# A hybrid decoder layer on eight cores: new start-up order and weight layouts, weight folds in two lanes, and a token mixer that begins inside the last FFN1 tiles

## The reference, cut to what matters

```python
def reference(x, c, w_ada, b_ada, ...):           # x (4, 8192, 1024) f32, D = 1024, D_FF = 2816
    mod = (silu(c) @ w_ada + b_ada).reshape(b, 9, D)      # shift, scale, gate for each of 3 sub-layers
    h = modulate(x, sh1, sc1)                             # layer norm without affine, * (1 + scale) + shift
    y = swiglu(h, ffn1_w_gate, ffn1_w_up, ffn1_w_down)    # (silu(h @ gate) * (h @ up)) @ down
    x = layer_norm(ALPHA * x + 0.5 * g1 * y, ln1_g, ln1_b)
    h = modulate(x, sh2, sc2)
    y = token_mix(h, w_in, attn_sinks, pool_w_mix, pool_scale, w_out)
                                                  # window-128 attention with sinks ++ causal pooling, @ w_out
    x = layer_norm(ALPHA * x + g2 * y, ln2_g, ln2_b)
    h = modulate(x, sh3, sc3)
    y = swiglu(h, ffn2_w_gate, ffn2_w_up, ffn2_w_down)
    return layer_norm(ALPHA * x + 0.5 * g3 * y, ln3_g, ln3_b)
```

## Time and profile before

| | |
|---|---|
| median of 3 runs | 2553.81 us (2540.72 to 2639.39) |
| the profiled execution's own time | 2549.48 us |
| its span on the slowest core (core 4) | 2547.9 us (the cores: 2518.9 to 2547.9) |
| PE busy | 2278.3 us, 89% of the span |
| DVE, ACT, POOL busy | 54%, 29%, 17% |
| mean granted PE clock, core 4 | 0.978 |

### The profile page before, as it was taken

One profiled execution on the slowest core, in us unless ns is written; L12 is line 12 of the kernel. 1 busy time (PEld: TensorE's weight loads), 2 busy tenths in 40 slices (PEclk: granted clock), 3 DMA queues, 4 the chain that ended last, 5 costly groups with the idle time before them and its releaser, 6 DMA issues.

```text
span 2547.9 us, 42339 instructions; the slowest of 8 cores (2518.9 to 2547.9 us)
## 1 busy us (share of the span) xinstructions
PE 2278.3 (89%) x14236; PEld 1286.2 (50%) x14360; DVE 1374.3 (54%) x2756; ACT 730.5 (29%) x1523; POOL 430.6 (17%) x422
## 2 busy tenths in 40 slices
PE   0069977988989999999789999999999999999997
PEld 0035543545545555565345555555555555555555
DVE  0064423442455533424767667776867676677654
ACT  0021211221221222212343334433333434343321
POOL 3100131222201110101111111202121111111111
PEclk9999989989999999999889999999999999999999
DMA  9963178997654311223515555454655555454556
GB/s 156 156 169 85 67 104 142 156 156 131 142 152 134 128 34 52 73 100 109 181 63 194 183 182 191 166 199 153 216 183 182 194 178 201 177 199 165 200 185 221
DMA packets 138358, 385.88 MB, mean 151 GB/s; under 512 B 19616, under 2 KB 71584, under 8 KB 116640
## 3 DMA queue, kind: packets, MB, share of 16 engines
q1 hardware_dynamic: 73152, 338.45, 39.2%
q0 software_dynamic: 64992, 44.70, 14.9%
HBM read 385.86 MB, written 56.11 MB: 173 GB/s over the span
## 4 chain that ended last, share of the span: by engine, by line
PE 74%; DMA 11%; DVE 5%; issue 5%; another core or an unknown queue 2%; POOL 1%; ACT 1%; SPq 0%; DVEq 0%; POOLq 0%; ACTq 0%
PE ps L1130 24%; PE ps L472 16%; PE ps L1153 12%; PE ps L539 8%; DMA t_arena<-ffn_w_down 4%; DMA t_arena<-w_ada 3%; PE ps L941 3%; PE ps L911 2%; PE ps L1061 2%; PE ps L1059 2%; DVE t_arena L647 2%; PE ps L426 2%; DMA scr_gu<-ffn_w_up 1%; DMA scr_win<-w_in 1%
## 5 line engine op out<-in xcount | busy, mean ns | idle before, releaser
L472 PE MATMUL ps<-t_arena 128*128 128x384 bf16 x3872 | 650.4, 330 | 20.8 <-DVE t_arena L463 16.1
L1130 PE MATMUL ps<-t_arena 128*128 128x384 bf16 (+1 forms) x3872 | 637.8, 322 | 1.8 <-DVE t_arena L410 1.8
L472 PEld LDWEIGHTS ps<-t_arena 128*128 128x128 bf16 x3872 | 378.5, 99 | 276.3 <-issue 36.2
L1130 PEld LDWEIGHTS ps<-t_arena 128*128 128x128 bf16 x3872 | 371.5, 98 | 243.6 <-issue 23.1
L386 ACT ACTIVATE t_arena<-t_arena,t_stt 128x1024 f32<-128x1024 f32 (+1 forms) x195 | 241.4, 1240 | 427.8 <-DVE t_stt L381 421.6
L379 POOL TENSOR_TENSOR t_stt<-t_stt,t_mhalf 128x1 f32<-128x1 f32 x195 | 114.1, 585 | 1440.8 <-DVE t_stt L378 1430.5
L463 DVE TENSOR_TENSOR t_arena<-ps,t_sg 128x384 bf16<-128x384 f32 x242 | 133.4, 556 | 367.1 <-PE ps L472 345.5
L539 PE MATMUL ps<-t_arena 128*128 128x512 bf16 x1413 | 319.6, 384 | 6.2 <-DVE t_arena L463 3.9
L1153 PE MATMUL ps<-t_arena 128*128 128x512 bf16 x1358 | 303.6, 379 | 3.1 <-issue 0.8
L495 POOL TENSOR_TENSOR t_arena<-t_arena 128x1024 f32<-128x1024 f32 x97 | 231.2, 2383 | 420.7 <-DVE t_arena L494 410.5
L375 DVE BATCH_NORM_STATS2 t_stt<-t_arena 128x6 f32<-128x512 f32 x390 | 269.4, 691 | 48.9 <-DMA t_arena<-x_c 24.1
(11 more groups left out here) (74 smaller groups left out, 1495.9 us busy)
## 6 DMA issues: line engine op xcount, KB each, us to landing
t_arena<-scr_gu SPq DMA_DIRECT2D x121, 1024.0 KB, 6.9
t_arena<-scr_d SPq DMA_DIRECT2D x44, 1024.0 KB, 5.6
t_arena<-x_c SPq DMA_DIRECT2D x66, 512.0 KB, 5.5
t_arena<-scr_x SPq DMA_DIRECT2D x65, 512.0 KB, 6.1
t_arena<-ffn_w_down SPq DMA_DIRECT2D x44, 512.0 KB, 4.6
scr_x<-t_arena SPq DMA_DIRECT2D x33, 512.0 KB, 3.3
t_arena<-scr_d SPq DMA_DIRECT2D x22, 768.0 KB, 4.5
out_c<-t_arena SPq DMA_DIRECT2D x32, 512.0 KB, 4.4
```

Of the source, the lines that this page charges most:

```text
L472: ins = e.matmul(bk.f[:, 0:T], lhsT=w.ap[:, kc, gu, s2 * 128:(s2 + 1) * 128], rhs=hT.ap[:, kc, 0:T], start=(kc == 0), stop=(kc == 7))
L1130: ins = e.matmul(bk.f[:, 0:T], lhsT=wv[:, kc, gu, s2 * 128:(s2 + 1) * 128], rhs=hTc.ap[:, kc, 0:T], start=(kc == 0), stop=(kc == 7))
```

## The change: what it does

1. **Layouts.** `w_ada`, `w_in`, `w_out` and both FFNs' gate and up weights arrive rearranged from the host, so that every weight DMA reads and writes long contiguous pieces: one DMA per chunk of gate and up instead of two, one cast for `w_in` instead of 17, 11 casts for FFN2 instead of 22.
2. **Start-up order.** The seven small constants go out on ACT's DMA queue instead of SP's. POOL issues 8 + 7 DMAs and then takes its first x^-0.5. Section 2 of `w_ada` loads after chunk 6, chunks 7 to 10 follow it. A block is loaded and its statistics taken before a destination buffer is free (`take_n2`, `box`). Six buffers instead of three take the rows of `ffn1_w_down`. Tile 0's down projection walks the 22 row blocks outermost in six PSUM banks (`down_first`), so it needs them one after another.
3. **Gate vector.** It is stored in plain order, element by element (1024 pieces of 4 bytes), so that the fold reads it with stride 1.
4. **Background.** The fold of `w_out` runs as a stream beside the sections; the fold of `ffn2_w_down` runs in two lanes; the casts begin after the last section. Consumers of background DMAs are placed as if the DMA landed 3 to 10 us later (`lag`). The model of DMA time is changed: separate queues, 285 KB/us alone, 150 KB/us beside another queue, at most 16 POOL DMAs outstanding.
5. **Mixer start.** `hTm0`, an own tile for the first mixer input, and other places for LN2's parameters and two of the x buffers let projections of tiles -1 and 0 stand among S9's gate and up matmuls and the first attention blocks among S9's down matmuls. Until FFN1 ends, one of the six weight buffers is free instead of three.

The core of the diff:

```diff
@@ Prog.emit
-            self.free_at[eng] = t + (0.9 if eng == "pool" else 0.1)
-            self.dma_at = max(self.dma_at, t) + op.nbytes / 280e3
-            self.fin[ev] = self.dma_at + 2.0
+            if eng == "pool":
+                if len(self.sw) >= 16:
+                    t = max(t, self.sw[-16])
+                self.free_at[eng] = t + 0.9
+            else:
+                self.free_at[eng] = t + 0.4
+            t0 = max(self.dma_at[eng], t)
+            busy = any(self.dma_at[o] > t0 for o in ENG if o != eng)
+            self.dma_at[eng] = t0 + op.nbytes / (150e3 if busy else 285e3)
+            self.fin[ev] = self.dma_at[eng] + 2.5
@@ load_small
-                yield dmaq("sp", dst, src, s_const, (), [B_const], 32768)
+                yield dmaq("act", dst, src, s_const, (), [], 4096)
@@ ada_section (gate)
-                yield dmaq("sp", scr_gate[gate], gtmp[:, gate, :], s_g, [B_g], [B_gd], 4096)
...
+                gd = scr_gate[gate].rearrange("a (j p) -> (a p) j", p=128)
+                yield Op("sp", lambda e: e.dma_start(out=gd, in_=gtmp[:, gate, :], allow_slow_non_contiguous=True), [B_g], [B_gd], 0.1, s_g, 262144)
@@ fold_op
-            return Op("dve", lambda e: e.scalar_tensor_tensor(out=v3(out), in0=v3(src), scalar=scale, in1=gview(gt), op0=ALU.mult, op1=ALU.mult),
-                      rd, wr, 1.25)
+            return Op("dve", lambda e: e.scalar_tensor_tensor(out=out, in0=src, scalar=scale, in1=gt.ap, op0=ALU.mult, op1=ALU.mult),
+                      rd, wr, 1.25, lag=lag)
@@ load_gu1
-                for gu in range(2):
-                    src = (wg[0], wu[0])[gu][:, j * 256:(j + 1) * 256].rearrange("(kc p) n -> p kc n", p=128)
-                    yield dmaq("pool", wgu[j].ap[:, :, gu, :], src, wgu[j].sem(), (), [wgu[j].buf] if gu == 0 else [], 1048576)
...
+                if j == 7:
+                    flags.add("gu1_some")
+                    yield from until("g1loads")
+                yield gu_load(j)
@@ bg_work
+            S.spawn(fold_wout(), 3)
             for sec, slot in ((3, 2), (4, 3), (6, 4), (7, 5)):
                 yield from ada_section(sec, adas, slot=slot)
+            yield from until("wout")
             yield from ada_section(8, adas, gate=2, gate_tile=gateb)
...
+            flags.add("ada_done")
+            for ln in range(2):
+                S.spawn(fold_wd2(ln), 3)
@@ casts
-            yield from until(("S0", "down", 1))
...
+            yield from until("ada_done")
+            jobs = [(scr_win, w_in, 5 << 20, None)]
             for j in range(NGRP):
...
+                jobs.append((scr_gu[j], wgu_d[1][j], 1 << 21, j))
@@ p1_main
-            yield from until("wd1_all", ("S0", "aT", 0, 21), ("S0", "aT", 1, 21))
-            for t in range(2):
-                yield from down1(t, aTs[t], "S0")
+            yield from down_first(aTs[0])
+            yield from until("wd1_all")
+            yield from down1(1, aTs[1], "S0")
@@ m_main
-            yield from until("att_mem", ("msc", 2), ("msc", 3))
-            S.spawn(m_pre(-1, [0], (("S9", "gu"),)), 2)
+            yield from until("casts", ("msc", 2), ("msc", 3), ("t1", 10, "hT"))
+            S.spawn(m_pre(-1, [0], ()), 2)
```

282 lines of the change are left out of this document (166 added, 116 removed).

## The result

The changed kernel takes **2564.9 us** (median of 13 runs), the kernel before 2543.4 us beside it. The ratio is 1.008, 95% interval 1.006 to 1.010, so it is no faster, rather 0.8% slower; forecast were 2381 us. Some executions of most kernels here, the one before too, run up to 17% longer with a lower granted clock on the cores of one die; the ratios, and the time given for cast_16k, leave these out, the other medians are of all executions. The busy times hardly moved against the earlier trace rows: PE is busy as long as before, and the time is again PE's idle time.

What follows compares the result with a forecast made beforehand. PE was taken as the bound, its 270 us of idle time and lower clock as the possible gain. 53 + 131 + 60 + 663 + 1472 = 2379 us of span, plus 1.6, gave 2381 us, range 2335 to 2450.

Steps and rivals of the forecast that it cites:

- What bounds the kernel: Whole kernel: PE is the bound, busy 2278 of 2548 us; to gain are its 270 us idle and lower-clock losses.
- Term 1: Start of S0, the first gate and up matmul: from 140.3 to 53 us, bounds 47 and 77.
- Term 2: S0's gate and up matmuls: 131 us, was 136.0.
- the gate vector: Its store as 1024 pieces in S0: 5 us, bounds 2.85 and 23, covered by PE's matmuls.
- Term 3: S0's down projections: 60 us, was 58.3; tile 2 begins at 244 us.
- Rival A: S0: the gate vector's store takes eight times as long, PE waits 9 to 13 us, 2392 us in all; chance 0.08.
- Term 4: Tiles 2 to 8 with the background work: 663 us, was 713.3, with 30 us of waits left; bounds 639 and 733.
- Rival B: Tiles 5 to 7: casts starve SP's transfers, x comes late, PE loses 40 to 60 us, about 2431 us; chance 0.15.
- Rival C: Tiles 2 to 8: lags and lanes do nothing, all 72 us of idle time stay, 2431 us; chance 0.10.
- Term 5: From S9 to the end: 1472 us, was 1500.0; mixer start hidden, second-half tiles stay at 119.65 us; bounds 1466 and 1500.
- Rival D: Second half: new DMA prices reorder FFN2's weight stream; 16 us lost per tile would cancel the gain; chance 0.05.
- The sum: Whole kernel: the five terms give a span of 2379 us, with 1.6 us added 2381 us, 6.8% less.

Runs made afterwards that it cites:

- cast_16k: The changed kernel with its 12 casts split into pieces of 16 KB read and 8 KB written: 2552.2 and 2555.6 us, two executions, no ratio.
- sem_only: gate_and_cast with an own semaphore for the first three constants and the first use of sinkt moved after tile 1's transposes: 2474.9 us.
- gate_contig: The changed kernel with the gate vectors' old HBM layout, 128 pieces of 32 bytes, the fold reading with a stride: 2524.5 us.
- cast_4k: The changed kernel with its 12 casts split into pieces of 4 KB read and 2 KB written instead of 64 and 32 KB: 2539.7 us.
- gate_and_cast: The changed kernel with both edits, gate_contig and cast_4k; base of several later kernels: 2498.7 us.
- paced: gate_and_cast with the same casts held back in the emitted order to places in tiles 5 to 8: 2464.1 us.
- all_five: gate_and_cast with paced, pn_lag, the first constants' own semaphore, later first use of sinkt, and tile 1's x in other buffers: 2416.9 us.
- gate_on_pool: all_five with the second and third gate vector stored and broadcast from POOL's queue instead of SP's: 2408.1 us.
- hard_pace: gate_on_pool with each cast waiting for the last matmul that stands ahead of it in the plan: 2402.1 us.
- late_lane: hard_pace with the second fold lane starting at tile 7 and both lanes drawing from one list of 22 folds: 2385.9 us.
- pn_lag: gate_and_cast with DVE's multiply of the attention weights planned at 2.1 us instead of 1.13, nothing else: 2478.1 us.

## Why the prediction was wrong, step by step

**What bounds the kernel** was right: PE's idle time was the whole of it, and all that the experiments gave back came from there.

**Term 1 (S0 at 53 us)** failed on a wait that I had not priced. "I take 53" counts w_ada and the first chunk, and both prices were good: w_ada landed at 40.7 us in sem_only (44 forecast), and chunks 7.0 us apart in the changed kernel and 6.2 in sem_only (6.5 forecast). It took for granted that DVE and ACT begin when x is there, as DVE did in the kernel before, at 7 us. But the change moved the first use of a constant ahead of the layer norms, and the seven constants share a semaphore and land one by one between w_ada's loads, the last at 29 us. With that wait gone S0 starts at 47. No row of the kernel before could show it, since the wait was not there; the new order of the lists could.

**Term 2 and the gate vector.** The store cost 22 us on core 3 and 16.1 on core 4. I had bounds of 2.85 and 23 and took 5 "since 128 pieces are mostly the fixed time of a DMA". Even if that is true of 128 pieces, it is no argument for 1,024: the upper bound, each piece at its old cost, was the right one. The rule that I had weighed says the same of the number of pieces: by the Trainium skill (DMA: Bandwidth & Descriptors, Rules for kernel authors) a strided last dim becomes one descriptor per element. The trace agrees: the changed kernel moves 2,688 more pieces of under 512 bytes than gate_contig, which is 3 x (1,024 - 128). S0 from gate and up to tile 2 took 200 us instead of 191; with the old layout 188.5 to 193.5, so **Term 3** and the rest of Term 2 stood. Rival A was right in its place and about right there (9 us). It priced only the first of three stores: the other two stood in SP's list ahead of x and ffn_w_down, 25.1 and 54.4 us. All three were worth 40 us, and two of them were in Term 4, where "SP stands still" had no number.

**Term 4 (tiles 2 to 8, 663 us)** is the largest miss: 772 on core 3, 757 on core 4, above even my upper bound of 733. (The lower bound that I gave, 639, is 643 by my own sum.) The step that failed is "30 us of waits left": PE stood idle for 134 us there on core 3. Rival B, together with the stores, is what happened, at twice its price. I gave it 0.15 "since tiles 5 to 7 had spare DMA time"; that was the mean of a stretch, but the casts went out as one burst, 601 to 781 us, right after the last section, beside two fold lanes. I priced a late x; what was late was ffn_w_down, on which DVE stood with PE's evacuations behind it. Of PE's 88.3 us in two waits one was the third gate vector, the other a load of 63 us.

As the mean of the eight cores, tiles 2 to 8 took:

| kernel | tiles 2 to 8, us | what is away |
|---|---|---|
| changed | 766.7 | |
| gate_contig | 729.2 | the stores |
| cast_4k | 748.4 | the long pieces |
| gate_and_cast | 705.3 | both |
| paced | 665.0 | also the burst |
| all_five | 672.2 | also the wait at the start, and the late multiply |
| gate_on_pool | 662.2 | also SP's stops for a gate vector |
| hard_pace | 656.4 | casts held back by a real wait |
| late_lane | 641.9 | also the second lane beside the casts |

So the last of these kernels is 21 us under my 663: the work needed no more, the waits did. Why all_five has 7 us more than paced is not known.

The rule named beside Rival B, that of the Trainium skill (DMA: Bandwidth & Descriptors, Queues, rings and completion order), is that an engine changes queues only at packet boundaries. The trace agrees in part: 64 KB pieces gave loads of 63 us and 4 KB ones 28.7 in the same burst, but 16 KB pieces still gave 62.8. It says nothing of the burst, which cost more.

Rival C did not happen: PE's waits for w_ada fell from 31.1 to 9.9 us on core 4, and on core 3 gate_contig has none in these tiles. Whether the lags did this or the new layout of w_ada, no run separates.

**Term 5 (S9 to the end, 1472 us)** failed twice. The mixer's start gained a part: from S9 to the second tile of FFN2 core 4 went from 378.1 to 369.4 us, 9 where I had asked for 28, with a wait of 10.0 us of the transposes for the last layer norm (L442 for ACT) where I had left 6 us in all. And "the second half's tiles stay at 119.65 us" was wrong: 121.3. It is Rival D in kind, at 2 us a tile and by another way than I wrote: not late weights, but PE's transposes moved up against DVE's multiply, about half of it by the planner's new DMA prices. The order before and after showed it on paper (no matmul between), beside a wait of 1.1 us at 8 matmuls. pn_lag brought back 119.0 us a tile and 1494 on core 3 (1498 on core 4, which had 1500 before); the other 22 us of the term are mostly the mixer's start.

**The sum.** The miss is 2565 - 2381 = 184 us. By the times of the kernels the wait at the start is worth 24 to 31, the stores 40, short pieces 25, spreading 35, the multiply 21, the store's queue 9, hard_pace 6 and the late second lane 16: 176 to 183. By the ratios the last two are 17 and 9, so only their sum, 22 to 25, is firm. Each part was measured once in one order of adding; where they add within 5 us (gate_and_cast, all_five) that is shown, for the last three it is the order in which they were made.

That late_lane stands at 2386, so near the forecast, is partly luck, for its terms (core 3) miss both ways:

| | forecast | changed | late_lane |
|---|---|---|---|
| start of S0 | 53 | 76 | 47 |
| S0 | 191 | 200 | 191 |
| tiles 2 to 8 | 663 | 772 | 639 |
| S9 to the end | 1472 | 1513 | 1497 |

Not settled: how the 35 us of spreading divide between casts against each other and casts against the fold lanes, what tightened the other half of the second half's order, and why the mixer's start gives only 9 us.

## What to carry to other kernels

Where a change only moves work, follow each queue for the first thing that will be late, and price a burst by what is in flight together, never by the stretch's mean share. A step that shares a semaphore, or stands in an in-order list ahead of what others need, can hold them as long as the slowest thing that it waits for: here a 2 KB constant cost 28 us of the start, and a 4 KB vector held a list for 54. Before a wait is blamed on a slow load, look when that load was issued. And when a planner's prices change, look at the order of the part that the change does not mean to touch, since that is where this one lost some 20 us, with no edit to the instructions there.

## What the runs showed of the hardware that I had not expected

- 4 KB stored as 1,024 pieces of 4 bytes took 15 to 25 us without casts in flight and 47 to 57 beside them (all eight cores of the changed kernel); as 128 pieces of 32 bytes 2.0 to 5.5 us, and 32 to 37 beside the same casts (gate_contig), 10 to 12 beside casts in 4 KB pieces (gate_and_cast).
- Beside the casts the DMA engines' share was 0.93 while 111 GB/s moved (750 to 800 us), where the second half moves 180 at 0.51, and another queue's 0.5 MB load took 63 us. With 16 KB pieces it was still 62.8, with 4 KB pieces 28.7. The high share alone is not the long pieces': with 4 KB ones it was 1.04 at 82 GB/s from 600 to 650 us.
- Small loads were not served sooner than large ones: the 2 KB load of pool_scale on ACT's queue, issued at 5.1 us, landed at 29.1, between the 1 MB loads of w_ada on POOL's that had landed at 28.9 and 32.4.
- With the waits gone the granted clock rose without anything else: over tiles 2 to 8 it was 0.91 in the changed kernel and 0.99 in late_lane.
